# Two transformer blocks with sixteen experts on one core: the second block's norms, attention and expert slots in another order

## The reference

```python
x = x + merged @ w_out                              # end of block 1
gate = sigmoid(rms_norm(x, norm_ple_g) @ w_ple_gate)
x = x + gate * (p @ w_ple_proj)                     # gate / proj groups
x = rms_norm(x, norm_final_g)
h = rms_norm_2(x, norm_mix_g_2); z = h @ w_in_2     # block 2
y_a = mlstm_branch(z) @ w_up_a                      # forward and backward scans in chunks of 128
y_b = diff_attention_branch(z) @ w_up_b             # 4 heads x 2 maps of 512x512, a = p0 - lam*p1
x = x + (sigmoid(z_ga) * y_a + sigmoid(z_gb) * y_b) @ w_out_2
aff = softmax(rms_norm_2(x, norm_ffn_g) @ w_router) # 16 experts
g, idx = top_k(aff.T, 64)                           # each expert takes 64 tokens
ye = (silu(xe @ w_gate_e) * (xe @ w_up_e)) @ w_down_e * g
x = rms_norm_2(x.at[idx].add(ye), norm_f_g)
```

## Time and profile before

| what | value |
|---|---|
| runs | 2097.86, 2092.34, 2097.74 us, median 2097.74 |
| profiled execution | 2091.48 us, its span 2089.4 us |
| busy PE / PEld | 1934.3 (93%) / 1146.5 us (55%) |
| busy DVE / ACT / POOL | 725.9 (35%) / 523.4 (25%) / 80.5 us (4%) |
| moved by DMA | 505.37 MB, mean 242 GB/s, of it HBM read 499.82 MB |
| chain that ended last | PE 62%, DMA 28%, DVE 4%, ACT 3% |

### The profile page before, as it was taken

How to read it: one execution, slowest core, us unless ns; L and a number is a source line. 1 busy time by engine, 2 the same in 40 slices (tenths; PEclk the granted TensorE clock), 3 DMA queues, 4 the chain that set the end, 5 groups by cost and what they waited for, 6 DMA issues and landing times.

```text
span 2089.4 us, 20846 instructions
## 1 busy us (share of the span) xinstructions
PE 1934.3 (93%) x8754; PEld 1146.5 (55%) x8754; DVE 725.9 (35%) x1121; ACT 523.4 (25%) x816; POOL 80.5 (4%) x67
## 2 busy tenths in 40 slices
PE   7999999999999899899986999988888898888897
PEld 6777788888877777677863333322222232222232
DVE  6534544333456775666443111101111111011111
ACT  4443422322245442456622000000000000000001
POOL 2000000000014401000000000000000000000000
PEclk9999999999999999999998999999999999999999
DMA  4221133233323222212554999999999999999996
GB/s 164 89 91 51 61 131 101 93 100 100 103 81 111 91 80 73 91 61 65 193 217 159 419 418 416 417 416 416 418 419 419 416 416 417 417 417 419 418 417 276
DMA packets 100012, 505.37 MB, mean 242 GB/s; under 512 B 10240, under 2 KB 10752, under 8 KB 66768
## 3 DMA queue, kind: packets, MB, share of 16 engines
q1 hardware_dynamic: 99600, 503.88, 61.4%
q10 hardware_dynamic: 320, 0.17, 0.0%
HBM read 499.82 MB, written 4.19 MB: 241 GB/s over the span
## 4 chain that ended last, share of the span: by engine, by line
PE 62%; DMA 28%; DVE 4%; ACT 3%; SPq 1%; issue 1%; POOL 1%; ACTq 0%; DVEq 0%; POOLq 0%
PE ps L1784 37%; DMA ring_a<-in_w_up_e 10%; PE ps L2102 9%; DMA ring_a<-in_w_gate_e 7%; DMA ring_b<-in_w_up_e 6%; DMA ring_b<-in_w_gate_e 4%; PE ps L2113 3%; PE ps L1743 3%; PE ps L2085 2%; SPq L610 1%; PE ps L2063 1%; PE ps L1958 1%; PE ps L1835 1%; PE ps L1832 1%; PE ps L1934 1%
## 5 line engine op out<-in xcount | busy, mean ns | idle before, releaser
L2102 PE MATMUL ps<-ring_a,xe 128*64 128x512 f32 x1376 | 318.2, 599 | 50.6 <-DMA ring_a<-in_w_up_e 35.2
L1102 DVE TENSOR_TENSOR d_lo<-d_raw,d_hi 128x1024 fp32r<-128x1024 f32 x168 | 210.6, 1263 | 113.8 <-ACT d_hi L735 113.3
L2102 PEld LDWEIGHTS ps<-ring_a,xe 128*64 128x64 f32 x1376 | 90.9, 136 | 275.4 <-issue 165.2
L2102 PE MATMUL ps<-ring_b,xe 128*64 128x512 f32 x672 | 156.8, 600 | 28.2 <-DMA ring_b<-in_w_up_e 20.4
L1291 DVE TENSOR_TENSOR hid<-sg,ps 128x512 f32<-128x512 f32 x32 | 20.6, 684 | 466.2 <-PE ps L2102 466.2
L1784 PE MATMUL ps<-n_hi,d_hi 128*128 128x512 f32 x448 | 175.6, 392 | 1.5 <-DVE d_lo L1102 0.8
L735 ACT ACTIVATE d_hi<-d_raw 128x1024 fp32r<-128x1024 f32 x168 | 173.0, 1049 | 10.2 <-DMA d_raw<-in_tiles_in 9.5
L1784 PE MATMUL ps<-n_hi,d_lo 128*128 128x512 f32 x448 | 174.5, 389 | 0.0
L1784 PE MATMUL ps<-n_lo,d_hi 128*128 128x512 f32 x448 | 174.4, 389 | 0.0
L1665 DVE TENSOR_TENSOR x<-x,ps 128x1024 f32<-128x1024 f32 x60 | 69.2, 1215 | 271.6 <-PE ps L2085 271.6
L2113 PE MATMUL ps<-ring_a,hidT 128*64 128x512 f32 x688 | 156.1, 597 | 6.1 <-ACT hidT L1080 3.9
(11 more groups left out here) (421 smaller groups left out, 2684.3 us busy)
## 6 DMA issues: line engine op xcount, KB each, us to landing
ring_a<-in_w_gate_e SPq DMA_DIRECT2D x88, 1024.0 KB, 20.9
ring_a<-in_w_down_e SPq DMA_DIRECT2D x86, 1024.0 KB, 23.2
d_raw<-in_tiles_in SPq DMA_DIRECT2D x168, 512.0 KB, 3.4
ring_a<-in_w_up_e SPq DMA_DIRECT2D x84, 1024.0 KB, 27.1
ring_b<-in_w_up_e SPq DMA_DIRECT2D x44, 1024.0 KB, 27.0
ring_b<-in_w_down_e SPq DMA_DIRECT2D x42, 1024.0 KB, 23.3
ring_b<-in_w_gate_e SPq DMA_DIRECT2D x40, 1024.0 KB, 21.1
x_in<-in_xT_in SPq DMA_DIRECT2D x4, 512.0 KB, 6.6
```

Source lines behind the costliest of these rows:

```text
L1102: dve.tensor_tensor(d_lo[:, n % SLOTS, :, :], d_raw[:, n % SLOTS, :, :], d_hi[:, n % SLOTS, :, :].bitcast(F32), ALU.subtract).then_inc(t_l ...
L2102: mm = pe.matmul(ps[half * CAP:(half + 1) * CAP, 2 * m + q, :], xe[:, k, :], slot(e, n)[:, (2 * q + half) * S:(2 * q + half + 1) * S], sta ...
```

## The change

**Norms by token.** For the gate stage and for the two final norms PE now makes token sums by four or eight products with one column of ones, into columns of a bank; scale, root and reciprocal work on [128, 4] or [128, 8]; DVE makes a diagonal (ident times the column) and PE multiplies ones with it, which gives the wide row that is copied to R. rf is spread in the same way in ub (diagonal at ub 0, product at ub 1, copy at ub 3).

**Order of groups.** gate 2 stands ahead of proj 7. dk 0 to 3 stand behind dq, ahead of mv; dq and dk read f_hi/f_lo (before the norm), and R is multiplied in when DVE reads the bank. part2/low2 (with POOL's x3 work gone to one DVE operation per out2 group) and the log gates are spread over dq 0 to mv 2. Splits of dq and dk stand ahead of the eviction. The x3 spill waits for the last low2.

**Slots.** dk no longer carries steps; every ua group does instead of every second one. mlstm_scale stands ahead of the attention step; the first bias map is made in mlstm_norm. g2a 0 and 1 go to a new buffer graw, and the others wait for what lay where they go.

**Last branch.** ub uses six banks; the addition goes to POOL for ub 0 to 6; the low part of ub i-1 is made at ub i; out2 0 waits for each low part by itself.

**Experts.** RING = 19; slot 19 (ring_c) lies where sg was, silu is written into hid. It is loaded behind the router's transposes. In the last expert place_turned follows gate_up 8, three residual products follow gate_up 9, 11 and 13, hidden_turned goes to banks 0 and 1, four residuals follow down 1 to 4.

**Decays.** Their first argument and exponentials move from v 4 to za 3.

The core of the diff:

```diff
-RING, RING_A = 18, 12
+RING, RING_A, RING_B = 19, 12, 6
...
     proj(6, 2)
+    gate(2)
     proj(7, 3)
-    for i in range(2, 8):
+    for i in range(3, 8):
         gate(i)
...
         columns("dq", i, "w_in_2", OFF_DQ + P * i, bank=(5, 6, 7, None)[i])
+    for i in range(4):
+        columns("dk", i, "w_in_2", OFF_DK + P * i)
     values("mv", 0, "w_in_2", OFF_MV)
...
-    halves("ub", "w_up_b_2")
+    halves("ub", "w_up_b_2", (0, 1, 4, 5, 6, 7))
...
-SLOT = [("dk", i) for i in range(4)] + [("dv", i) for i in range(4)] + [("mo", i) for i in range(4)]
-SLOT += [("g2a", i) for i in range(8)] + [("ua", i) for i in (1, 3, 5, 7)] + [("g2b", i) for i in range(8)]
+SLOT = [("dv", i) for i in range(4)] + [("mo", i) for i in range(4)]
+SLOT += [(name, i) for name in ("g2a", "ua", "g2b") for i in range(8)]
...
+NORMED = {("dq", 0): [0], ("dq", 1): [1, 2], ("dq", 2): [3, 4], ("dq", 3): [5, 6], ("dk", 0): [7]}
...
-            pool.wait_ge(fn_dve.sem, fn_dve.count("rf"))
-            for k in range(KD):
-                x3_pool.done(pool.tensor_tensor(x1[:, k, :], x1[:, k, :], rf[:, :], ALU.mult), f"r{k}")
-                x3_pool.done(pool.tensor_scalar(x1[:, k, :], x1[:, k, :], vcol("final", k), None, ALU.mult), f"x{k}")
...
+            for i in range(KD - 1):
+                mb_pool.done(pool.tensor_tensor(gbl[:, i, :], gbl[:, i, :], glog(i), ALU.add), f"m{i}")
...
+                elif (name, i) == ("za", 3):
+                    decays()
                 elif (name, i) == ("v", 4):
-                    decays()
+                    decay_inverse()
...
-                    for k in range(KD):
+                elif (name, i) in NORMED:
+                    for k in NORMED[name, i]:
                         n2_act.done(act.activation(h_hi[:, k, :], scr[2 + k % 2][:, 0:S], ACT.Copy), f"hi{k}")
+                    if (name, i) == ("dq", 0):
+                        gate_bias()
+                    elif (name, i) == ("dq", 1):
+                        gate_logs()
-                elif (name, i) == ("mv", 1):
-                    gate_logs()
-                elif (name, i) == ("mv", 3):
+                elif (name, i) == ("mv", 0):
                     gate_rows()
+                elif (name, i) == ("mv", 2):
+                    row_exps()
...
-                elif name in ("mg", "dq"):
+                elif name in ("mg", "dq", "dk"):
                     hi, lo = f_hi, f_lo
...
                     if k == FIRST_F - 1:
                         mlstm_moments()
+                        mlstm_scale()
...
-                    if k == FIRST_F - 1:
-                        mlstm_scale()
...
-                    r_one.done(pe.matmul(ps[:, 7, :], ones[:, :], pacc[:, :], start=True, stop=True), "sum")
+                    for t in range(TT):
+                        mm = pe.matmul(ps[:, 7, t:t + 1], pacc[:, t * P:(t + 1) * P], ones[:, 0:1], start=True, stop=True)
+                    r_one.done(mm, "sum")
+                elif (name, i) == ("gate", 0):
+                    r_one.done(pe.matmul(ps[:, 7, :], ones[:, :], dg[:, :, :], start=True, stop=True), "R")
```

More of the change, by code:

```diff
@@ L89, in halves @@
                 tiles.append(("half", w, P * i))
-            add(name, i, nk=4, k0=i % 2 * 4).tiles = [len(tiles) - 1]
+            add(name, i, nk=4, bank=banks[i % len(banks)], k0=i % 2 * 4).tiles = [len(tiles) - 1]
     for i in range(4):
@@ L1587, in _ @@
                     splits(gr)
-                    norm_rows()
-                    part2(0)
-                    for k in range(KD):
-                        if k + 1 < KD:
-                            part2(k + 1)
-                        low2(k)
-                    group_done(dve, gr)
-                    dve.tensor_tensor(gates[:, :], ps[:, gr.bank, :], R[:, :], ALU.mult).then_inc(t_ev[gr.bank], 1)
+                    final_norm()
                     continue
+                early = gr.name in ("dq", "dk")
+                if early:
+                    splits(gr)
                 evict(gr)
@@ L1609, in _ @@
                     p_dve.done(low(pT_lo[:, k, :], pT_raw[:, k, :], pT_hi[:, k, :]), f"lo{k}")
-                splits(gr)
+                if not early:
+                    splits(gr)
                 if gr.name == "gate":
@@ L1717, in group1 @@
                 elif (name, i) == ("proj", 5):
-                    pe.wait_ge(pr_act.sem, pr_act.count("root"))
-                elif (name, i) == ("mg", 0):
-                    for n in range(2, 8):
-                        read_done(pe, "proj", n)
-                elif (name, i) == ("out2", 0):
-                    pe.wait_ge(mb_dve.sem, mb_dve.count("lo", KD - 2))
+                    pe.wait_ge(pr_dve.sem, pr_dve.count("R"))
                 elif (name, i) == ("ua", 0):
@@ L2129, in _ @@
             gather_turned(0)
-            for e in range(NE):
+            for e in range(NE - 1):
                 pe.wait_ge(x_dve.sem, x_dve.count("xe", e))
@@ L2164, in _ @@
-            pe.wait_ge(e_act.sem, e_act.count("ye", NE - 1))
+            e = NE - 1
+            pe.wait_ge(x_dve.sem, x_dve.count("xe", e))
+            gate_up(e, 0)
+            placed(e - 1)
+            for n in range(1, 2 * KD):
+                if n == KD:
+                    pe.wait_ge(e_dve.sem, e_dve.count("o2", e - 1))
+                gate_up(e, n)
+                if n == 8:
+                    pe.wait_ge(e_dve.sem, e_dve.count("o1", e - 1))
+                    last_pe.done(place_turned(e), "place")
+                elif n == 9:
+                    pe.wait_ge(e_dve.sem, e_dve.count("o3", e - 1))
+                    residual(2, 0, 6)
+                elif n == 11:
+                    residual(2, 1, 7)
+                elif n == 13:
+                    pe.wait_ge(last_act.sem, last_act.count("place"))
+                    residual(3, 1, 5)
@@ L2165, in _ @@
+            last_pe.done(hidden_turned(e, 0), "hT")
+            pe.wait_ge(last_act.sem, last_act.count("hT0"))
+            pe.wait_ge(e_dve.sem, e_dve.count("hT1", e))
+            for i in range(8):
+                down(e, i)
+                if 1 <= i <= 4:
+                    residual((i - 1) // 2, (i - 1) % 2, i - 1)
+            pe.wait_ge(last_act.sem, last_act.count("ye"))
             for t, banks in enumerate(((0, 1), (2, 3), (6, 7))):
                 for d in range(2):
-                    mm = put(NE - 1, t, d, banks[d], False)
```

348 lines of the change are left out of this document (218 added, 130 removed).

## The result

The changed kernel takes 2077.48 us (median of 4 runs, 2076.26 to 2079.75), the kernel before 2095.54 us (4 runs, one more than was known before). The ratio is 0.9917, with a 95% interval from 0.9901 to 0.9933. The profiled execution took 2076.26 us, against 2091.48.

What follows compares the result with a forecast made beforehand. Bound: TensorE's own stream until about 1140 us, then DMA engines full at 417 GB/s. Terms sum to -10.1 us from 2091.5, so 2081.4; plus 6.2 for the runs' median, given as 2087; range 2069 to 2102, forecast's own 2079 to 2095.

Steps and rivals of the forecast that it cites:

- the 20 and 17 among my signs: Tail: the last down tile was to come about 17 us after the last up tile's matmuls instead of 20.
- The norms and dq to mqk: Gate norm -1.1, mg group -0.4, dq to mqk -7.4 (-11.9 for removed waits and slow matmuls, +4.5 for new waits).
- The loop: Each ua slot's product waits for aaT, copied after the previous slot's exponentials: +1.0 us in each of eight slots, 8.0.
- Rival A: ua stage: the attention loop hides, so the +14.4 goes and the time is 2073; chance 0.17.
- Rival B: VectorE bounds dq to dk and ub, port lockout with GpSimd being of this kind; gains mostly go: 2098, no change; chance 0.2.
- Rival C: ua stage: waits make TensorE's clock fall, +4.2 a slot, +33 in all eight: 2120, slower; chance 0.07.
- D: Experts: the 19th slot or moved residuals gain nothing as transfers end later; 5.7 less gain, 2093, the same; chance 0.05.
- "-2.8" for the decays: First block: moving two exponentials to za 3 removes TensorE's 2.84 us wait for the read of a v group: -2.8.
- Attention: ua groups: loop 8.0, sigmoids after g2a 7 +2.6, heads' ends +3.8; sum +14.4, bounds nothing and 17.
- moments: mLSTM scaling ahead of the attention: -6.0 for hn's wait and slow scores, +3.2 before a later transposition; sum -2.8.
- The last branch: End of g2b to out2: six banks let TensorE run on, -5.3; GpSimd's seven additions beside VectorE +1.0; sum -4.3.
- The gate and mg: Norm sums as one-column matmuls taken as even with before; spreading product +1.0 each; gate -1.1, mg -0.4, its slow stretch gone.

## Why the prediction was right and wrong

**Right.** The bound: 417 GB/s in the expert part, one megabyte less 2.4 us (forecast 2.5), three residuals 3.1 (3.2). From the last up tile's matmuls to the last down tile it is 20.2 us after 23.8 before (2051.05 to 2074.89); the 20 and 17 among my signs were misread, the difference nearly right. **The norms and dq to mqk** came out at -9.3 where I had -8.9 (the table's +0.4, -5.2 and -4.5), in part by luck: the new waits of 4.5 in dq to mqk are only one of 1.67, for dqT and not for dk's banks, but 1.7 to 2.2 at half clock stand behind the wait for facc, which I had at nothing. **The loop** in ua: eight waits, 0.6 to 0.8 in seven of them and 3.3 in ua 1, by the mechanism as I had put it. Rival A (it hides) fell, although the time came out near the 2073 that I gave for it: right number, wrong reason. Rival B fell, with the ten microseconds for its port rule: seven additions on GpSimd cost the 1.0 that I had added for them (0.7 by the medians). Rival C did not come: the granted clock over the ua stage (913 to 971.5 us) was 0.97 of full. D fell.

**The size was wrong**, -10.1 as a sum where the stages gave -15.0, and two terms of the sum are at fault before the others.

**The first step that failed is "-2.8" for the decays**, and with it the rule by which I priced most removed waits: the idle time that the row shows. Only for the wait ahead of mqk (3.1) and for hn's (the slow scores) did I count what ran slow behind it. It is not an accident of those places. A wait of 2.45 was worth 5.2 to 5.8, one of 2.84 about 6 in the changed kernel (3.9 in its own stage) and 4.2 in the one before; the table has -4.3 for it. In the profile that I read, the wait for v_tok happened to have full clock behind it (window 131 to 135.5 above), and half clock at 72 us, which other executions of it don't have.

**Attention was mis-sized the other way, and by more**: +14.4 against 9.9 by the medians and 11.4 by the stage. The mechanism was right, the size not. The wait of a slot is 0.6 to 0.8, not 1.0; ua 1 waits 3.3 instead of 3.6; a head's end 1.4 instead of 1.9. With the **moments** the stage has +9.6 where I had +11.6. Taking 11.4 for the attention leaves about -1.8 for them, where I had -2.8: hn's wait of 5.04 is gone, and 1.49 for dsm and 0.75 for aa came instead of 3.2 before one transposition. No run undoes them alone.

**The last branch was nearly right in size for a wrong reason**: -4.3, measured -5.3 from ub 0 to out2 (30.0 to 24.7 us). 3.6 to 4.0 of it is the low part moved a group later. The six banks on which I had put it are worth nothing, and GpSimd costs 1.0.

**The gate and mg.** I had TensorE sums even with before. Sixteen one-column products took 1.8 us at full clock and 2.93 where the clock had fallen, and I had expected the slow stretch behind the mg wait to go; it stayed, behind another wait.

**The scale.** I set the profile 6.2 us under a median of three runs. Over 9 to 15 runs a batch the kernel before is at 2093.2 to 2094.9, some 3 us lower. Of the 10.1 us between 2087.6 and 2077.5 the terms are 5 by the table. About 3 are this median. The other 2 are that the kernel before lies some 2 us above the mean of its two profiles in its medians, the changed one 0.6 us; why, no run shows.

What stays open: I have not undone the new place of the mLSTM's scaling, of gate 2 or of dk, nor the norms by token. Why the wait for v_tok costs about 6 us in one kernel and 4.2 in the other is not shown; the intervals allow that it is the same.

## What to carry to other kernels

Where TensorE sets the end, price a removed wait of two to four microseconds at its length and some 1.5 to 2 us more for the stretch at half clock that stood behind most of them here, and look at the granted clock behind it in more than one profile, since one profile is one draw. To price an edit, compare the stage in which it stands as well as the medians: here the two differed by up to 2.3 us (6.2 against 3.9 for the decays, 9.9 against 11.4 for the attention), and the median takes in stretches that no edit touched. Before another engine or more buffers are given to a chain, look at its order: here a copy placed ahead of two exponentials, a sum half a group later and a low part one group later were worth 7.6, 5.2 and 4.0 us, six banks nothing, and GpSimd cost 1.0. When a part is undone to price it, look in the profile for waits that neither kernel has.

## What the runs showed of the hardware

Whether TensorE's clock is granted at half for a few microseconds differs between executions of one and the same program: 15 matmuls in the six microseconds from 72 us in one, 27 in the other; over the profiles read here the toll of such stretches goes from 0 to 10.2 us, and the executions of the kernel before are spread over 2089 to 2098 us. The half clock stood behind waits, but not behind each. One-column products took 0.10 us each at full clock (eight in 0.81 us, sixteen in 1.7 to 1.8) and 0.18 where the clock had fallen (sixteen in 2.93).

The Trainium skill ("SBUF — State Buffer", on the engine ports) has a VectorE operation with two inputs in SBUF and a GpSimd one that reads SBUF lock each other out: the first holds the ports for its whole instruction. The trace agrees in the rows shown above. The low part at 1048.26 us began while GpSimd's addition still had 0.56 us to go (1045.89 + 2.93 = 1048.82) and took 1.10 us instead of 0.69. The one at 1045.73 began ahead of the addition and took 0.69. The product at 1046.33, with one input in PSUM, took its usual 0.68 beside the addition. GpSimd's addition behind that low part, which began 0.16 us after it, took 1.67 us where others take 1.30. The loss is small because only three of the eight low parts began during an addition, in its last 0.6 us at most (0.78, 1.11 and 1.10 us).
